# Softmax division ahead of the transposes in a hybrid encoder: weights divided on GpSimd, value products with features on partitions

## The chip, the cores and the metric

The kernel runs on one core of one Trainium2 chip. The metric is the device time of one execution in microseconds, lower is better. The core has TensorE (PE in the rows, with its weight loads as PEld), VectorE (DVE), ScalarE (ACT), GpSimd (POOL) and SyncE (SP, which only starts DMAs here).

## The reference, cut to what matters

The program is one inference step of two layers for 256 prompt tokens and 32 sample tokens. Between two large feed-forward blocks each layer mixes tokens with three groups of heads; the change concerns the first group, forgetting attention of the prompt tokens:

```
def fox_block(q, k, v, cq, ck, mask):
    s = jnp.einsum('bqhd,bkhd->bhqk', q, k).astype(F32) * (HEAD_DIM ** -0.5)
    s = s + jnp.swapaxes(cq, 1, 2)[:, :, :, None] - jnp.swapaxes(ck, 1, 2)[:, :, None, :]
    s = jnp.where(mask[None, None], s, -jnp.inf)
    p = jax.nn.softmax(s, axis=-1).astype(v.dtype)
    return jnp.einsum('bhqk,bkhd->bqhd', p, v)
...
    o_fox = (o_fox.reshape(B, T, FOX_WIDTH) * jax.nn.sigmoid(fg)).astype(x.dtype)
```

It has 8 heads of 64 features; `cq` and `ck` are running sums of log forget gates; queries come in two blocks of 128, of which the first sees 128 keys and the second 256. The second group of heads (RWKV-7) carries a state of 64x64 per head through the sequence; the kernel computes it in nine chunks of 32 tokens, each of which needs the state that the one before left.

## The kernel before, in words

All tensors are feature-major: features on partitions, 288 tokens along the free axis. Each engine has one instruction stream, written by hand in program order; semaphores join them. In the part that the change touches the nine chunks of the recurrence run one after another, and the work of the forgetting heads is written between their parts. We call chunk i "step i", from 0 to 8.

A step of the recurrence is a chain of four links. TensorE multiplies the state by the chunk's vectors (L1769); VectorE adds the result to `u0` (L1206); TensorE adds two products for the new state (L1775, which needs nothing new, and L1782, which waits for `u0`); VectorE scales the old state and adds (L1213, two instructions). The next step's first product waits for that.

The forgetting heads go in four pairs p of heads 2p and 2p+1. The stages of a pair:

- `fox_scores(p)`, TensorE, L1701 and L1706: scores into PSUM banks 4 and 5, one for each head. It waits until the exponentials of the pair before have read them.
- `fox_max(h)`, VectorE, L1176: mask and row minimum of the negated scores, in two parts.
- `fox_exp(h)`, ScalarE, L691: exponentials of both parts into `pq`, with their row sums into `fm`. It waits until the transposes of head h-2 have read `pq`.
- `fox_weights(p)`, TensorE, L1731: three 128x128 transposes for each head into banks 6 and 7.
- `fox_copy(h)`, ScalarE, L701: copy of these from PSUM to `pt`.
- `fox_products(p)`, TensorE, L1743: six products of the weights (stationary, 128x128) with the values (64 columns), into bank 3, tokens on partitions.
- `fox_normed(p)`, VectorE, L1183 and L1184: reciprocal of the sums, product with them, to `otok`.
- `fox_back(p)`, TensorE, L1753: two transposes, so that features are on partitions again.
- `fox_out(p)`, VectorE, L1192: product with the gate into `hT`.

`fox_values` (L1717, copies L708) transposes the values once. Which stage stands behind which step is set by two tables named `meanwhile`, one in TensorE's stream and one in VectorE's (there with the part of the step: "u" behind L1206, "s" behind L1213). ScalarE's stream has no steps: it takes its work in the written order. `at_most` (L934) and two passes at L578 and L579 make the gate.

After step 8 TensorE computes the recurrence's outputs (L1801, then L1813), four sums for a norm (L1821), and the scores of the sample tokens (L1835), and so on to the output projection (L1882). GpSimd starts a few DMAs in this stretch.

Of the kernel before, what the change touches and what calls it, by code (L numbers as in the profile page):

```python
# [79 lines left out]
for _name, _n in (("n1", DB), ("nm", DB), ("n2", DB), ("pn", DB), ("mu", 7), ("prev", 7), ("bf", 1), ("w0", 2),  # L80
# [29 lines left out]
    fexp=16, ft_ps=8, ftc=8, fo_ps=4, fno=4, ft2=4, fo_ok=4, ss_ps=2, smx=2, sexp=4, st_ps=4, stc=4, so_ps=1,  # L110
# [19 lines left out]
def program(nc, wcol, x_in, p_in, consts_in, params_in, foxl_in, kc_in, vc_in, clf_in, srwkv_in, sret_in,  # L130
            nf_in, y_out, k_out, v_out, logf_out, shift_out, rwkv_out, ret_out):
    with ExitStack() as ctx:
# [231 lines left out]
        with nc.Block() as block:  # L364
# [42 lines left out]
            def _(pool):  # L407
                for layer in range(DEPTH):
# [42 lines left out]
                    pool.dma_start(ret_out[layer, 1], rst[:, 6, :, :]).then_inc(S["zstore"], 16)  # L451
                    pool.wait_ge(S["s_ok"], past["s_ok"] + 18)
# [14 lines left out]
            def _(act):  # L467
                n_chain = [0]
                for layer in range(DEPTH):
# [241 lines left out]
                    for p in range(4):  # L711
                        for e in range(2):
                            fox_copy(2 * p + e)
                        if p < 3:
                            for e in range(2):
                                fox_exp(2 * p + 2 + e)
# [100 lines left out]
            def _(dve):  # L817
                n_chain = [0]
                for layer in range(DEPTH):
# [359 lines left out]
                    def fox_normed(p):  # L1179

                        dve.wait_ge(S["fo_ps"], past["fo_ps"] + p + 1)
                        total = 12 + 4 * (p % 2)
                        link(dve.reciprocal(fm[:, 20:24], fm[:, total:total + 4]))  # L1183
                        dve.tensor_tensor(otok, bank[3][:, 0:256].rearrange("p (a d) -> p a d", a=4),  # L1184
                                          fm[:, 20:24].unsqueeze(2).to_broadcast([P, 4, HD]), ALU.mult).then_inc(S["fno"], 1)

                    def fox_out(p):

                        if p == 0:
                            dve.wait_ge(S["fg_ok"], past["fg_ok"] + 1)  # L1190
                        dve.wait_ge(S["ft2"], past["ft2"] + p + 1)
                        dve.tensor_tensor(hT[:, p, 0:TP], bank[3][:, 256:512], fg[:, p, 0:TP], ALU.mult).then_inc(S["fo_ok"], 1)  # L1192

                    meanwhile = {(0, "u"): [(fox_max, 0)], (0, "s"): [(fox_max, 1)], (1, "s"): [(at_most, fg)],
                                 (2, "u"): [(fox_max, 2)], (2, "s"): [(fox_max, 3)], (3, "u"): [(fox_normed, 0)],
                                 (4, "u"): [(fox_out, 0)], (4, "s"): [(fox_max, 4)], (5, "u"): [(fox_max, 5)],
                                 (5, "s"): [(fox_normed, 1)], (6, "s"): [(fox_out, 1)], (7, "u"): [(fox_max, 6)],
# [945 lines left out]
```

## Time and profile before

| what | us |
|---|---|
| median of 3 runs | 1439.85 (1438.88 to 1444.85) |
| the profiled execution, its own time | 1437.9 |
| its span | 1436.1 |
| TensorE busy | 1367.6 (95%) |
| VectorE busy | 864.2 (60%) |
| ScalarE busy | 597.0 (42%) |
| GpSimd busy | 49.3 (3%) |

The span is what the trace covers; the profiled execution took 1.8 us more. TensorE is busy nearly throughout, most of it in the feed-forward blocks. The stretch with the nine steps stands once in each layer, at 382 to 429 us and at 1096 to 1137 us of the span.

### The profile page before, as it was taken

The page shows a single profiled execution, that of the slowest core. Times are in us where ns is not written, and L with a number is a line of the kernel's source. Part 1 is how long each engine was busy: PE and PEld are TensorE (multiplying, and loading weights), DVE is VectorE, ACT ScalarE, POOL GpSimd, SP SyncE. Part 2 cuts the span into 40 slices and gives each one's busy share as a digit, 9 for nine tenths or more (in the row PEclk, how much of TensorE's full clock was granted, in tenths as well). Part 3 has the DMA queues.
Part 4 walks back from the last instruction along what each step waited for, and adds up shares of the span by engine and source line. Part 5 has one row for each costly group of instructions (what it writes and reads, how often), then busy time and mean ns, then how long its engine had stood idle before and what let it go on. Part 6 is the DMA issues. An engine that isn't in the chain of part 4 may idle for free.

```text
span 1436.1 us, 29222 instructions
## 1 busy us (share of the span) xinstructions
PE 1367.6 (95%) x12544; PEld 1317.7 (92%) x12544; DVE 864.2 (60%) x1365; ACT 597.0 (42%) x845; POOL 49.3 (3%) x71
## 2 busy tenths in 40 slices
PE   6999999998898999999999999999989899999997
PEld 6999999898777999999989999998977699999996
DVE  5766536796346566653766664467853565766546
ACT  5443434533326544433544343335333364443333
POOL 1000000003100000000000000000031100000000
PEclk9999999999779999999999999999997899999999
DMA  8444443434103344444444444523432035444440
GB/s 315 166 175 157 165 171 122 147 122 152 65 14 118 147 162 160 175 154 169 151 151 176 154 168 173 178 90 120 163 110 64 14 118 199 153 175 156 167 146 34
DMA packets 31328, 205.29 MB, mean 143 GB/s; under 512 B 4312, under 2 KB 5864, under 8 KB 7544
## 3 DMA queue, kind: packets, MB, share of 16 engines
q1 hardware_dynamic: 28672, 195.62, 37.9%
q0 software_dynamic: 2560, 8.26, 1.7%
q8 instruction: 75, 1.23, 0.3%
q14 instruction: 21, 0.17, 0.0%
HBM read 199.77 MB, written 4.10 MB: 142 GB/s over the span
## 4 chain that ended last, share of the span: by engine, by line
PE 88%; DVE 4%; ACT 4%; issue 2%; DMA 1%; POOL 0%; SPq 0%; DVEq 0%; ACTq 0%
PE banks L1390 40%; PE banks L1413 19%; PE banks L1465 11%; PE banks L1919 3%; PE banks L1882 3%; PE banks L1887 1%; PE banks L1701 1%; PE banks L1900 1%; PE banks L1743 1%; PE banks L1643 1%; PE banks L1821 1%; PE banks L1706 1%; ACT split_h L572 1%; PE banks L1631 1%; PE banks L1731 0%
## 5 line engine op out<-in xcount | busy, mean ns | idle before, releaser
L1390 PE MATMUL banks<-split_x,split_w 128*128 128x288 f32 x4224 | 570.5, 297 | 16.2 <-ACT split_x L492 11.8
L1390 PEld LDWEIGHTS banks<-split_x,split_w 128*128 128x128 f32 x4224 | 567.4, 190 | 18.8 <-issue 11.7
L844 DVE TENSOR_TENSOR split_w<-wc,split_w 128x2048 fp32r<-128x2048 f32 x139 | 318.6, 2292 | 346.5 <-ACT split_w L508 346.5
L508 ACT ACTIVATE split_w<-wc 128x2048 fp32r<-128x2048 f32 x139 | 266.4, 1916 | 401.0 <-PE banks L1390 207.4
L1413 PE MATMUL banks<-split_x,split_w 128*128 (+1 forms) x2112 | 282.3, 295 | 0.0
L1413 PEld LDWEIGHTS banks<-split_x,split_w 128*128 128x128 f32 x2112 | 281.8, 188 | 0.0
L1465 PE MATMUL banks<-split_h,split_x 128*128 128x288 f32 x752 | 115.7, 301 | 5.7 <-ACT split_x L566 4.2
L1465 PEld LDWEIGHTS banks<-split_h,split_x 128*128 128x128 f32 x752 | 105.9, 191 | 9.0 <-DVE zT L939 5.4
L566 ACT ACTIVATE split_x<-wc 128x1024 fp32r<-128x1024 f32 x62 | 65.1, 1057 | 112.2 <-PE banks L1465 97.2
L533 ACT ACTIVATE et<-hT 128x288 f32<-128x288 f32 x88 | 35.5, 445 | 110.4 <-DVE hT L863 110.3
L1465 PE MATMUL banks<-split_x 128*128 128x288 f32 x496 | 76.9, 298 | 0.0
L1465 PEld LDWEIGHTS banks<-split_x 128*128 128x128 f32 x496 | 70.2, 191 | 0.0
L1919 PE MATMUL banks<-split_x,split_w 128*128 128x288 f32 x384 | 53.0, 297 | 0.0
L1919 PEld LDWEIGHTS banks<-split_x,split_w 128*128 128x128 f32 x384 | 51.7, 189 | 1.1 <-ACT split_x L784 1.1
L939 DVE TENSOR_TENSOR zT<-banks,rs 128x288 f32<-128x288 f32 x62 | 28.1, 454 | 33.0 <-PE banks L1465 24.1
L1465 PE MATMUL banks<-split_h,split_e 128*128 128x288 f32 x240 | 38.2, 302 | 7.5 <-DVE split_e L930 7.5
L868 DVE SCALAR_TENSOR_TENSOR et<-et,hT 128x288 f32<-128x288 f32 x88 | 36.4, 455 | 12.6 <-ACT et L533 9.1
L930 DVE TENSOR_TENSOR split_x<-wc,split_x 128x1024 fp32r<-128x1024 f32 x32 | 39.0, 1218 | 7.8 <-ACT split_x L566 7.8
L874 DVE SCALAR_TENSOR_TENSOR et<-et,banks 128x288 f32<-128x288 f32 x88 | 39.3, 450 | 4.8 <-PE banks L1390 3.5
L1465 PEld LDWEIGHTS banks<-split_h,split_e 128*128 128x128 f32 x240 | 34.4, 193 | 8.4 <-DVE split_e L930 8.4
L930 DVE TENSOR_TENSOR split_e<-wc,split_x 128x1024 fp32r<-128x1024 f32 x30 | 36.5, 1217 | 6.8 <-ACT split_x L566 6.8
L863 DVE TENSOR_TENSOR hT<-banks,rs 128x288 f32<-128x288 f32 x88 | 35.9, 449 | 5.9 <-ACT rs L487 5.9
(290 smaller groups left out, 1194.6 us busy)
## 6 DMA issues: line engine op xcount, KB each, us to landing
wc<-wcol SPq DMA_DIRECT2D x182, 1024.0 KB, 4.8
arena<-kc_in POOLq DMA_DIRECT2D x8, 256.0 KB, 3.5
arena<-vc_in POOLq DMA_DIRECT2D x2, 1024.0 KB, 7.5
con<-consts_in SPq DMA_DIRECT2D x1, 1830.0 KB
xT<-x_in SPq DMA_DIRECT2D x2, 576.0 KB, 4.5
k_out<-zT POOLq DMA_DIRECT2D x8, 144.0 KB, 2.5
v_out<-zT POOLq DMA_DIRECT2D x8, 144.0 KB, 2.5
y_out<-hT SPq DMA_DIRECT2D x8, 144.0 KB, 1.9
```

The lines of the kernel that those rows point to most:

```text
L508: act.activation(ws[(s + 1 - f) % 2][0], wc[:, p % RING, :], ACT.Copy).then_inc(S["cast"], 1)
L566: act.activation(zw[n % 2][0], z_raw(n), ACT.Copy).then_inc(S["zcast"], 1)
L844: dve.tensor_tensor(lo, wc[:, (POS_FFN[f] + s) % RING, :], hi, ALU.subtract).then_inc(S["wlo"], 1)
L863: dve.tensor_tensor(half[:, q % 2, :], bank[2 * (q % 4)][:, 0:T], rs[:], ALU.mult)\
L868: dve.scalar_tensor_tensor(e, e, 1.0, half[:, q % 2, :], ALU.add, ALU.mult)\
L874: dve.scalar_tensor_tensor(e, e, 0.5, bank[2 * (q % 4) + 1][:, 0:T], ALU.mult, ALU.mult)\
L930: dve.tensor_tensor(lo, z_raw(n), hi, ALU.subtract).then_inc(S["zlo"], 1)
L1390: mm = pe.matmul(o, w[:, k, cs], x[:, k, :], start=(n == 0 and k == 0), stop=(n == 2 and k == DB - 1))
L1413: return pe.matmul(bank[m][:, 0:T], w[:, kk, m * 128:m * 128 + 128], rhs, start=start, stop=stop)
L1465: mm = pe.matmul(o, w[:, k, :], zh_lo(k) if second else zh_hi[:, k, :], start=(i == 0 and k == 0), stop=(i == 2 and k == DB - 1))
L1882: pe.matmul(bank[2 * s + cc][:, 0:T], hi[:, k, cc * 128:cc * 128 + 128], x[:, k, :], start=(x is oh_hi and k == 4), stop=False)
L1919: mm = pe.matmul(bank[2 * s + cc][:, 0:T], w[:, k, cc * 128:cc * 128 + 128], x[:, k, :], start=(n == 0 and k == 0), stop=(n == 2 and k == ...
```

## The change

The softmax's division moves from behind the value products to ahead of the transposes. VectorE now takes the reciprocal of a head's two sums as soon as its exponentials are there (`fox_inverse`), and GpSimd multiplies the head's exponentials by them, in place (`fox_divide`). The transposes wait for GpSimd in place of ScalarE. The value products are turned round: the values are stationary (128x64), the weights move, 256 and 128 columns at a time, and the two heads of a pair write to the two halves of bank 3's partitions. Features are then on partitions at once, so `fox_normed` and `fox_back` are gone, and `fox_out` reads the products directly. The tables give some stages other steps, and ScalarE takes the exponentials of the next pair between the copies of a pair, where it took them behind both.

```
...
         pool.dma_start(ret_out[layer, 1], rst[:, 6, :, :]).then_inc(S["zstore"], 16)
+        def fox_divide(h):
+            p, e = h // 2, h % 2
+            pool.wait_ge(S["frc"], past["frc"] + h + 1)
+            for part, (a0, a1) in enumerate(((0, 128), (128, 384))):
+                one = 20 + 4 * (p % 2) + 2 * part + e
+                done = pool.tensor_scalar(pq[:, e, a0:a1], pq[:, e, a0:a1], fm[:, one:one + 1], None, ALU.mult)
+            done.then_inc(S["fpn"], 1)
+        for h in range(FOX_H):
+            fox_divide(h)
         pool.wait_ge(S["s_ok"], past["s_ok"] + 18)
...
             for e in range(2):
+                if p < 3:
+                    fox_exp(2 * p + 2 + e)
                 fox_copy(2 * p + e)
-            if p < 3:
-                for e in range(2):
-                    fox_exp(2 * p + 2 + e)
...
-        def fox_normed(p):
-            dve.wait_ge(S["fo_ps"], past["fo_ps"] + p + 1)
-            total = 12 + 4 * (p % 2)
-            link(dve.reciprocal(fm[:, 20:24], fm[:, total:total + 4]))
-            dve.tensor_tensor(otok, bank[3][:, 0:256].rearrange("p (a d) -> p a d", a=4),
-                              fm[:, 20:24].unsqueeze(2).to_broadcast([P, 4, HD]), ALU.mult).then_inc(S["fno"], 1)
+        def fox_inverse(h):
+            p, e = h // 2, h % 2
+            dve.wait_ge(S["fexp"], past["fexp"] + 2 * h + 2)
+            at = 4 * (p % 2) + e
+            dve.reciprocal(fm[:, 20 + at:23 + at:2], fm[:, 12 + at:15 + at:2]).then_inc(S["frc"], 1)
         def fox_out(p):
             if p == 0:
                 dve.wait_ge(S["fg_ok"], past["fg_ok"] + 1)
-            dve.wait_ge(S["ft2"], past["ft2"] + p + 1)
-            dve.tensor_tensor(hT[:, p, 0:TP], bank[3][:, 256:512], fg[:, p, 0:TP], ALU.mult).then_inc(S["fo_ok"], 1)
-        meanwhile = {(0, "u"): [(fox_max, 0)], (0, "s"): [(fox_max, 1)], (1, "s"): [(at_most, fg)],
-                     (2, "u"): [(fox_max, 2)], (2, "s"): [(fox_max, 3)], (3, "u"): [(fox_normed, 0)],
-                     (4, "u"): [(fox_out, 0)], (4, "s"): [(fox_max, 4)], (5, "u"): [(fox_max, 5)],
-                     (5, "s"): [(fox_normed, 1)], (6, "s"): [(fox_out, 1)], (7, "u"): [(fox_max, 6)],
-                     (7, "s"): [(fox_max, 7)], (8, "u"): [(fox_normed, 2)], (8, "s"): [(fox_out, 2)]}
+            dve.wait_ge(S["fo_ps"], past["fo_ps"] + p + 1)
+            dve.tensor_tensor(hT[:, p, 0:TP], bank[3][:, 0:TP], fg[:, p, 0:TP], ALU.mult).then_inc(S["fo_ok"], 1)
+        meanwhile = {(0, "u"): [(fox_max, 0)], (0, "s"): [(fox_max, 1)], 
+                     (1, "s"): [(at_most, fg), (fox_inverse, 0), (fox_inverse, 1)],
+                     (2, "u"): [(fox_max, 2)], (2, "s"): [(fox_max, 3)], (3, "s"): [(fox_inverse, 2)],
+                     (4, "u"): [(fox_inverse, 3), (fox_out, 0)], (5, "u"): [(fox_max, 4)], (5, "s"): [(fox_max, 5)],
+                     (6, "u"): [(fox_inverse, 4), (fox_inverse, 5), (fox_out, 1)], (7, "u"): [(fox_max, 6)],
+                     (7, "s"): [(fox_max, 7)], (8, "u"): [(fox_inverse, 6)],
+                     (8, "s"): [(fox_inverse, 7), (fox_out, 2)]}
         dve.wait_ge(S["uac"], past["uac"] + 8)
...
         dve.tensor_copy(kc[:, :, PAST:], zT[:, Z_FK:Z_FK + 4, TP:T]).then_inc(S["kcnew"], 1)
-        fox_normed(3)
         by_chunk = ow[:, :, 0:TP].rearrange("p b (j c u) -> p c j b u", j=2, c=4)
...
                 h = 2 * p + e
-                pe.wait_ge(S["fexp"], past["fexp"] + 2 * h + 2)
+                pe.wait_ge(S["fpn"], past["fpn"] + h + 1)
                 if p:
...
                 pe.wait_ge(S["fo_ok"], past["fo_ok"] + p)
-            for e in range(2):
-                hv = slice(HD * (2 * p + e), HD * (2 * p + e) + HD)
-                for i, (q, kb) in enumerate(((0, 0), (1, 0), (1, 1))):
-                    at = 128 * q + 64 * e
-                    mm = pe.matmul(bank[3][:, at:at + HD], pt[:, e, 128 * i:128 * i + 128], vtok[:, kb, hv],
-                                   start=(kb == 0), stop=(kb == q))
+            for kb, (a0, a1) in enumerate(((0, 256), (256, 384))):
+                for e in range(2):
+                    hv = slice(HD * (2 * p + e), HD * (2 * p + e) + HD)
+                    mm = pe.matmul(bank[3][64 * e:64 * e + 64, 128 * kb:256], vtok[:, kb, hv], pt[:, e, a0:a1],
+                                   start=(kb == 0), stop=(kb == 1), skip_group_check=True)
             mm.then_inc(S["fo_ps"], 1)
-        def fox_back(p):
-            pe.wait_ge(S["fno"], past["fno"] + p + 1)
-            both = otok.rearrange("p a d -> p (a d)")
-            for q in range(2):
-                at = 256 + 128 * q
-                mm = pe.transpose(bank[3][:, at:at + 128], both[:, 128 * q:128 * q + 128], c("ident"))
-            mm.then_inc(S["ft2"], 1)
         fox_scores(0)
-        meanwhile = {0: [(fox_values,)], 1: [(fox_weights, 0), (fox_scores, 1)], 2: [(fox_products, 0)],
-                     3: [(fox_back, 0), (fox_weights, 1), (fox_scores, 2)], 4: [(fox_products, 1)], 5: [],
-                     6: [(fox_back, 1), (fox_weights, 2), (fox_scores, 3)], 7: [(fox_products, 2)],
-                     8: [(fox_back, 2), (fox_weights, 3)]}
+        meanwhile = {0: [(fox_values,)], 1: [(fox_scores, 1)], 2: [(fox_weights, 0)], 3: [(fox_products, 0)],
+                     4: [(fox_scores, 2), (fox_weights, 1)], 5: [(fox_products, 1)],
+                     6: [(fox_scores, 3), (fox_weights, 2)], 7: [(fox_products, 2)], 8: []}
         for i in range(NCH):
...
         mm.then_inc(S["o_in"], 1)
-        fox_products(3)
+        fox_weights(3)
         pe.wait_ge(S["o_in"], past["o_in"] + 1)
...
             mm.then_inc(S["o_ps"], 1)
-        fox_back(3)
+        fox_products(3)
```

ScalarE's stream from the copies of pair 0 to the exponentials of pair 2, before (L701 is a copy, L691 an exponential; 128x128 and 128x256 are a head's two parts):

```order
L701 ACTIVATE arena<-banks 128x384 [waits ft_ps] x2
L691 ACTIVATE arena<-banks,arena 128x128 [waits fmx,ft_ps]
L691 ACTIVATE arena<-banks,arena 128x256
L691 ACTIVATE arena<-banks,arena 128x128 [waits fmx,ft_ps]
L691 ACTIVATE arena<-banks,arena 128x256
L701 ACTIVATE arena<-banks 128x384 [waits fo_ps,ft_ps] x2
L691 ACTIVATE arena<-banks,arena 128x128 [waits fmx,ft_ps]
L691 ACTIVATE arena<-banks,arena 128x256
```

The same place after the change (L713 is a copy, L703 an exponential):

```order
L703 ACTIVATE arena<-banks,arena 128x128 [waits fmx,ft_ps]
L703 ACTIVATE arena<-banks,arena 128x256
L713 ACTIVATE arena<-banks 128x384 [waits ft_ps]
L703 ACTIVATE arena<-banks,arena 128x128 [waits fmx,ft_ps]
L703 ACTIVATE arena<-banks,arena 128x256
L713 ACTIVATE arena<-banks 128x384 [waits ft_ps]
L703 ACTIVATE arena<-banks,arena 128x128 [waits fmx,ft_ps]
L703 ACTIVATE arena<-banks,arena 128x256
L713 ACTIVATE arena<-banks 128x384 [waits fo_ps,ft_ps]
```

Before, both copies of pair 0 come ahead of all exponentials of pair 1. Now each copy stands behind the exponentials of the head two further on: the copy of head 0 behind those of head 2, and so on to the last row, the copy of head 2, behind those of head 4.

TensorE's stream from the products of pair 1 to step 6, before (L1769, L1775 and L1782 are a step, L1743 the products):

```order
L1743 MATMUL banks<-arena 128x64 [waits fo_ok,ftc]
L1743 MATMUL banks<-arena 128x64 x5
L1769 MATMUL banks<-extra,arena 32x64 [waits s_ok]
L1769 MATMUL banks<-extra,arena 32x64 x3
L1775 MATMUL banks<-extra 64x64 x4
L1782 MATMUL banks<-arena,extra 64x64 [waits u_ok]
L1782 MATMUL banks<-arena,extra 64x64 x3
L1769 MATMUL banks<-extra,arena 32x64 [waits s_ok]
L1769 MATMUL banks<-extra,arena 32x64 x3
L1775 MATMUL banks<-extra 64x64 x4
```

After the change, from step 5 on (L1753 are now the products):

```order
L1769 MATMUL banks<-extra,arena 32x64 [waits s_ok]
L1769 MATMUL banks<-extra,arena 32x64 x3
L1775 MATMUL banks<-extra 64x64 x4
L1782 MATMUL banks<-arena,extra 64x64 [waits u_ok]
L1782 MATMUL banks<-arena,extra 64x64 x3
L1753 MATMUL banks<-arena 64x256 [waits fo_ok,ftc]
L1753 MATMUL banks<-arena 64x256
L1753 MATMUL banks<-arena 64x128 x2
L1769 MATMUL banks<-extra,arena 32x64 [waits s_ok]
L1769 MATMUL banks<-extra,arena 32x64 x3
```

Before, the products of pair 1 come ahead of step 5, and step 6 follows it directly. After, step 5 is the first five rows, and the products stand between it and step 6. The products of pair 2 stand between steps 7 and 8 in both kernels.

TensorE's stream behind step 8, before (L1801 and L1813 are the recurrence's outputs, L1753 the transposes back, L1821 the norm's sums):

```order
L1801 MATMUL banks<-arena,extra 64x32 x2
L1801 MATMUL banks<-arena 64x32 x2
L1743 MATMUL banks<-arena 128x64 [waits fo_ok,ftc]
L1743 MATMUL banks<-arena 128x64 x5
L1813 MATMUL banks<-arena,extra 64x32 [waits o_in]
L1813 MATMUL banks<-arena,extra 64x32 x35
L1753 MATMUL banks<-con,arena 128x128 [waits fno]
L1753 MATMUL banks<-con,arena 128x128
L1821 MATMUL banks<-arena,con 128x288 [waits ftc]
L1821 MATMUL banks<-arena,con 128x288
```

After the change (L1742 are the transposes of the weights, L1753 the products):

```order
L1801 MATMUL banks<-arena,extra 64x32 x2
L1801 MATMUL banks<-arena 64x32 x2
L1742 MATMUL banks<-con,arena 128x128 [waits ftc,fpn]
L1742 MATMUL banks<-con,arena 128x128 x2
L1742 MATMUL banks<-con,arena 128x128 [waits ftc,fpn]
L1742 MATMUL banks<-con,arena 128x128 x2
L1813 MATMUL banks<-arena,extra 64x32 [waits o_in]
L1813 MATMUL banks<-arena,extra 64x32 x35
L1753 MATMUL banks<-arena 64x256 [waits fo_ok,ftc]
L1753 MATMUL banks<-arena 64x256
L1753 MATMUL banks<-arena 64x128 x2
L1821 MATMUL banks<-arena,con 128x288 [waits ftc]
```

The last pair's transposes have moved from ahead of L1801 to behind it, and its products from ahead of L1813 to behind it.

## Rows read from the trace of the kernel before

**Rows 1.** Windows of layer 0, then layer 1: length, busy time of each engine, clock, DMA

```profile
core 0: us, PE busy (x) PEld busy (x) DVE busy (x) ACT busy (x) POOL busy (x), PEclk, DMA share, GB/s
418.60:428.80 10.20, 10.20 (x98) 8.88 (x95) 4.30 (x12) 1.06 (x1) 0.54 (x1) 0.55 0.10 32
382.36:428.80 46.44, 42.15 (x582) 34.45 (x581) 20.88 (x82) 15.68 (x46) 1.61 (x3) 0.83 0.04 12
...
1123.10:1136.80 13.70, 13.19 (x310) 11.32 (x307) 7.57 (x29) 3.75 (x11) 1.61 (x3) 1.00 0.06 16
1095.64:1136.80 41.16, 37.97 (x582) 31.03 (x581) 20.02 (x81) 15.68 (x46) 1.61 (x3) 0.92 0.04 13
```

**Rows 2.** Waits of TensorE, 382.3 to 428.8 us: total, times, longest

```profile
PE banks L1801 <- issue: 1.2, 1, 1.2
PE banks L1731 <- ACT arena L708: 0.8, 1, 0.8
PE banks L1769 <- DVE extra L1213: 0.7, 1, 0.7
```

**Rows 3.** Timeline of step 7: start, duration, engine, line, operation, idle before and releaser

```profile
410.06 0.41 PE L1769 MATMUL banks<-extra,arena 64*32 64x64 f32 x8
...
410.52 0.43 DVE L1206 TENSOR_TENSOR arena<-arena,banks 32x256 f32<-32x256 f32 x1 [4.73 <-PE banks L1769]
410.98 0.30 DVE L1176 CUSTOM_DVE_ANT_0 banks<-banks,con 128x128 f32<-128x128 f32 x1
...
411.38 1.55 PE L1743 MATMUL banks<-arena 128*128 128x64 f32 x12
...
411.88 0.37 ACT L691 ACTIVATE arena<-banks,arena 128x128 f32<-128x128 f32 x1 [4.75 <-DVE arena L1176]
...
412.86 0.41 PE L1769 MATMUL banks<-extra,arena 64*32 64x64 f32 x8
```

**Rows 4.** Timeline of step 1 on ScalarE and VectorE, and a reciprocal of step 6

```profile
385.01 0.37 ACT L691 ACTIVATE arena<-banks,arena 128x128 f32<-128x128 f32 x1
...
385.81 1.52 ACT L708 ACTIVATE arena<-banks 128x512 f32<-128x512 f32 x3
386.12 0.45 PE L1782 MATMUL banks<-arena,extra 32*64 32x64 f32 x8
...
387.00 0.75 DVE L934 TENSOR_SCALAR zT<-zT 128x1152 f32<-128x1152 f32 x1
...
402.73 0.17 DVE L1183 RECIPROCAL arena<-arena 128x4 f32<-128x4 f32 x1
```

**Rows 5.** All copies L701: duration ns min/median/max, first and last start

```profile
L701 ACT ACTIVATE arena<-banks x16: 471/488/490, 390.1 to 1128.9; 128x384 f32<-128x384 f32 x16
```

**Rows 6.** Timeline of TensorE behind step 3, at the full clock

```profile
394.77 0.44 PE L1753 MATMUL banks<-con,arena 128*128 128x128 f32 x2 [0.22 <-DVE arena L1184]
...
395.04 0.82 PE L1731 MATMUL banks<-con,arena 128*128 128x128 f32 x6
...
395.70 1.48 PE L1701 MATMUL banks<-foxR,foxL 128*128 128x128 f32 x8
...
397.11 0.93 PE L1706 MATMUL banks<-zT 64*128 64x128 f32 x8
397.96 0.41 PE L1769 MATMUL banks<-extra,arena 64*32 64x64 f32 x8
```

**Rows 7.** Timeline of TensorE behind step 6, at half the clock

```profile
405.12 1.49 PE L1731 MATMUL banks<-con,arena 128*128 128x128 f32 x6
...
406.40 2.77 PE L1701 MATMUL banks<-foxR,foxL 128*128 128x128 f32 x8
```

**Rows 8.** Timeline of TensorE, layer 0: products in column and row tiles; layer 1: full tiles

```profile
432.57 1.15 PE L1843 MATMUL banks<-arena,zT 64*32 64x512 f32 x32
...
1134.86 2.11 PE L1821 MATMUL banks<-arena,con 128*128 128x288 f32 x8
```

**Rows 9.** GpSimd's multiplications by a per-partition scalar: duration ns min/median/max

```profile
L443 POOL TENSOR_SCALAR arena<-arena,par x4: 993/1195/1395, 350.2 to 1062.8; 128x288 f32<-128x288 f32 x4
```

More of the change, by code:

```diff
@@ L109 @@
     rsd=10, ro_ps=2, ro_ok=3, rgate=2, fu_ok=1, fl_ok=1, lgf_ok=1, fc_ok=3, vt_ps=3, vtc=3, fs_ps=8, fmx=16,
-    fexp=16, ft_ps=8, ftc=8, fo_ps=4, fno=4, ft2=4, fo_ok=4, ss_ps=2, smx=2, sexp=4, st_ps=4, stc=4, so_ps=1,
+    fexp=16, ft_ps=8, ftc=8, frc=8, fpn=8, fo_ps=4, fo_ok=4, ss_ps=2, smx=2, sexp=4, st_ps=4, stc=4, so_ps=1,
     son=1, sot=1, so_ok=1, gpre=2, kcnew=1, mixout=1, pchain=4, rwkv_done=1, ret_done=1, ocast=4, olo=4, oh_hi=3, oh_lo=3, pj_ps=8,
```

## The prediction

> **What bounds the kernel now.** The profile page has TensorE busy for 95% of the span, so I looked first at who ends its waits, and then at the one stretch that the change touches. There the windows show 42.15 us of TensorE work in 46.44 us in layer 0, and 37.97 in 41.16 in layer 1 [rows 1]. Its waits by releaser are few: 0.8 us for ScalarE's copies of the values, 0.7 for the state of step 6, and 1.2 of issue in L1801 [rows 2]. So VectorE and ScalarE are hidden, and TensorE's own time sets the length, if it isn't made to wait. The two layers do the same work with 5.3 us of difference; 1.2 of it is the issue gap, and about 4.1 is the clock: behind step 8 layer 0 has a granted clock of 0.55, close to the lower level of 1.2 GHz, and layer 1 has 1.00, which is 2.4 GHz [rows 1]. Both layers fall to the lower level once more, at step 6. There a pair's scores take 3.66 us (406.40 to 410.06) where they take 2.26 at the full clock (395.70 to 397.96), and the transposes 1.49 against 0.82 [rows 3, 6, 7]. With step 6 itself that is some 2.5 us in each layer. What a delay here costs, the end pays: behind the stretch TensorE goes on in written order, and no DMA limits what follows.
>
> **What TensorE no longer does.** The transposes back take 0.27 us a pair (394.77 to 395.04) [rows 6], 1.1 us a layer. The products take 1.48 (411.38 to 412.86) [rows 3]. The new ones have as many moving columns in each pass as L1706, which runs in two row halves and takes 0.85 (397.11 to 397.96) [rows 6]: four matmuls, two of 256 and two of 128 columns, two passes each. If the two column halves do not run side by side, the price per column of L1821 holds, 2304 columns in 2.11 us, and 1536 columns take 1.4 [rows 8]. But L1843, in four column strips and two row halves, moves 16 passes of 512 and 16 of 32 columns in 1.15 us, a seventh of that price [rows 8], which row halves alone don't give. I take 0.86; 1.4 would add 4.3 us over both layers. So TensorE's work falls by 4 x 0.62 + 1.1 = 3.6 us a layer.
>
> **Waits that go.** The transposes of pair 0 no longer come ahead of the copies of the values (0.8), step 6 no longer follows step 5 directly (0.7) [rows 2], and `fox_back` no longer waits for `fox_normed` (0.2 at step 3 [rows 6], and as much behind step 8). A view counts idle from a matmul's modelled end, about 0.1 us late, so by starts it is 2.1 us a layer.
>
> **Waits that come.** The main one follows from ScalarE's new order. At step 5 TensorE stands at the products of pair 1 and needs the copies of heads 2 and 3; those stand behind the exponentials of heads 4 and 5, whose row minima VectorE takes in this same step. From the start of a step's first product to the first exponential of its scores is 1.82 us in the trace (410.06 to 411.88, over the add at 410.52 and the minimum at 410.98) [rows 3]. Exponentials hold ScalarE 0.80 (385.01 to 385.81) [rows 4], a copy takes 0.49 [rows 5]. So the copies are there 1.82 + 0.80 + 0.49 + 0.80 + 0.49 = 4.40 us after the step's start. TensorE has finished the step after 1.32 (410.06 to 411.38) [rows 3] and waits 3.1 us. The same stands at step 7 for the products of pair 2, which before ran at once, because the copies of pair 2 came ahead of the exponentials of pair 3. Behind the waiting products stands the next step of the recurrence, and behind that everything: 6.2 us a layer. At step 3 the exponentials come from a step earlier, and I count nothing.
>
> The second is GpSimd. One multiplication of 128x288 takes 0.993 at least [rows 9]. A head needs 128 and 256 columns in two instructions: 1.32 if all the time goes by columns, 1.99 if all goes by instruction. I take the middle, 1.65, and 3.3 for a pair. The first pair's reciprocals follow `at_most`, which ends at 387.75; with 0.2 for a reciprocal the divides end at 391.25. TensorE is at the second head's transposes at 386.12 + 0.4 + 2.26 for the scores + 1.32 for step 2 + 0.33 for the first head = 390.4 [rows 4], so it waits 0.9. For pair 2, from the start of step 6: add 0.46, next on VectorE 0.46, reciprocal 0.2, divides 3.3, together 4.4; TensorE takes 1.32 + 2.26 + 0.33 = 3.9 and waits 0.5. Pair 1's divides lie beside step 4 and the scores of pair 2, pair 3's beside L1801. With 1.99 the two waits grow by 0.7 each, 2.8 us over both layers; with 1.32 they nearly vanish, and the copy at step 3 takes half of that back. The reciprocals on VectorE replace those of `fox_normed` and lie beside TensorE's work.
>
> The Trainium skill (GPSIMD Engine Reference, 4.1 Engine selection) gives elementwise work to VectorE and calls GpSimd roughly line-rate for one input; 384 elements at its 1.2 GHz would be an estimate of 0.32 us a head, and the sum would be 2 us smaller. The trace's 0.993 for 288 speaks against that figure [rows 9].
>
> Third, L1801 used to stand behind the last pair's transposes, which covered the last state update. Now it follows step 8 and waits for it like step 6 did, 0.6 [rows 2]. GpSimd's output DMAs now stand behind the divides, and nobody waits for them in this stretch.
>
> **Sum at the clocks of before.** Per layer 6.2 + 0.9 + 0.5 + 0.6 = 8.2 us of new waits, less 2.1 of old ones, less 3.6 of work: 2.5. Both layers: +5 us.
>
> **The clock.** TensorE stands still for 3 us twice a layer, with only small tiles around it. In layer 0 of before the clock fell after the gap in L1801 and stayed low to 428.8; in layer 1, without the gap, it stayed full [rows 1, 2]. The wait at step 7 is followed by short work and then L1801, in both layers. So I expect the low clock behind step 8 in both: +4.1 in layer 1, and the last pair's transposes, which now lie there, +0.7 in each. The low clock around step 6 I expect as before, on the scores of pair 3 and the transposes of pair 2, which still stand there; TensorE is then so slow that it no longer meets the 0.5 of the divide, -1.0 over both layers. That makes +4.5. In all 1437.9 + 5 + 4.5 = 1447.4 for the profiled execution's own time. Its 1437.9 is 1.95 under the median of the runs, so **1449.5 us** is the forecast.
>
> **Rivals.** *The clock stays as it was* (chance 0.27): the waits come, but layer 1 keeps its full clock behind step 8. For it: there was no fall in layer 1, although TensorE's work was much the same. Then +5, 1445.
>
> *Full clock throughout, not slower* (0.07): scores of pair 1 now come without a wait, so wide matmuls stand closer together in the first steps, and the clock may hold in both layers. That takes back 2.5 in each layer and 4.1 in layer 0, 9.1 in all, against +5: 1436. It decides where both low stretches of layer 0 are gone; one alone doesn't. Against it: the new waits are the longest that TensorE would have in the stretch.
>
> *GpSimd is too slow* (0.09): another of the same multiplications took 1.395 [rows 9]. At that, a head costs 2.8 and a pair 5.6. Every pair's transposes then wait, by 2.3 us more a pair less what was covered, about 7 us a layer more: 1449.5 + 14 less some 2 of clock, 1461. It sets in at about 2 us a head; below that only two waits are touched. The Trainium skill (SBUF — State Buffer, Who interferes with whom) has GpSimd blocked only by VectorE instructions with two SBUF inputs or in a two-port mode. By that rule the divides would run free, since VectorE's work in the steps reads PSUM and one SBUF tensor, and this rival would fall.
>
> My own case, waits and low clock, has 0.5, with its own range 1445 to 1456; the remaining 0.07 is for what I don't see. A measurement of this kernel tells about 0.5%, 7.2 us, from no change. The own case is over that with 0.42 of its 0.5; slow divides all; the clock-as-before case mostly under it, 0.06 over, with products in series (1449) among the reasons. That gives slower 0.57, the same 0.37, faster 0.06. For the range I leave out the full-clock case and the slow end of the divides: 1441 to 1460.
>
> **What would show it.** Idle of about 3 us ahead of L1753 behind steps 5 and 7, ended by ScalarE's copy L713; products at about 0.86 us; 1.3 to 2.0 us of GpSimd a head; short waits of L1742 for L459; L1801 waiting about 0.6 for L1225; the granted clock near 0.5 behind step 8 in both layers. The forecast is wrong if the products wait under 2 us, if the clock differs, or if the divides exceed 2 us.

## The result, and the profile after

The changed kernel takes **1453.7 us** (median of 6 runs, 1449.2 to 1457.0) against 1440.3 for the kernel before (6 runs): ratio over the runs 1.0074, 95% interval 1.0048 to 1.0100 (the two medians alone stand at 1.0093). It is slower by some 0.7 to 0.9%. A second batch of 6 runs gave 1455.6 and 1.0093 (1.0062 to 1.0125). The forecast was 1449.5, with 1441 to 1460 as its range. The profiled execution after has an own time of 1449.61 us and a span of 1447.8, with a mean clock of 0.959; before it was 1437.9, 1436.1 and 0.968.

TensorE's waits of the changed kernel, 382.3 to 445 us, layer 0 (total, times, longest); layer 1 reads the same:

```profile
PE banks L1753 <- ACT arena L713: 6.4, 3, 3.0
...
PE banks L1801 <- DVE extra L1225: 0.6, 1, 0.6
...
PE banks L1742 <- POOL arena L459: 0.3, 1, 0.3
```

These stand against [rows 2]. The old waits of [rows 2] are gone, and TensorE now waits for ScalarE's copies, twice for 3 us and once, at step 3, for 0.44. The timeline around step 5, layer 0, tells why, and ends with the next step of the recurrence (start, duration, engine, line, operation, idle before and releaser):

```profile
401.20 0.87 PE L1742 MATMUL banks<-con,arena 128*128 128x128 f32 x6
...
402.00 0.41 PE L1769 MATMUL banks<-extra,arena 64*32 64x64 f32 x8
...
403.81 0.37 ACT L703 ACTIVATE arena<-banks,arena 128x128 f32<-128x128 f32 x1 [8.73 <-DVE arena L1187]
...
404.62 0.49 ACT L713 ACTIVATE arena<-banks 128x384 f32<-128x384 f32 x1
404.99 0.38 ACT L703 ACTIVATE arena<-banks,arena 128x128 f32<-128x128 f32 x1
...
405.78 0.51 ACT L713 ACTIVATE arena<-banks 128x384 f32<-128x384 f32 x1
...
406.34 0.87 PE L1753 MATMUL banks<-arena 128*64 128x256 f32 x8 [2.96 <-ACT arena L713]
...
407.14 0.64 PE L1769 MATMUL banks<-extra,arena 64*32 64x64 f32 x8
```

The transposes of pair 1 end when step 5 begins, at 402.0, and ScalarE stands idle; yet the copies of heads 2 and 3 come only at 404.62 and 405.78, behind the exponentials of heads 4 and 5, whose minima VectorE takes during step 5. The products take 406.34 to 407.14, 0.80 us. The next step already runs at the lower clock: 0.64 for what took 0.41 at 402.00.

The same wait at step 7, GpSimd's divides for the last pair, and the short wait for the last state:

```profile
418.79 1.55 PE L1753 MATMUL banks<-arena 128*64 128x256 f32 x8 [2.96 <-ACT arena L713]
...
421.53 3.00 POOL L459 TENSOR_SCALAR arena<-arena 128x128 f32<-128x128 f32 x4 [10.00 <-DVE arena L1195]
...
422.68 0.47 PE L1801 MATMUL banks<-arena,extra 32*64 32x32 f32 x16 [0.58 <-DVE extra L1225]
```

The windows of the whole stretch, from step 0 to the sample scores, in both layers, of the kernel after; its columns are those of [rows 1]:

```profile
384.20:435.44 51.24, 42.97 (x559) 32.14 (x558) 18.45 (x81) 15.16 (x46) 13.63 (x19) 0.73 0.05 17
1097.97:1148.68 50.71, 42.43 (x558) 31.72 (x557) 18.52 (x81) 15.15 (x46) 13.63 (x19) 0.73 0.06 19
```

Layer 1 in four pieces: up to the products behind the first long wait; steps 6 to 7; around the second wait; from its products on:

```profile
1097.97:1120.00 22.03, 17.45 (x220) 12.25 (x218) 10.38 (x48) 10.63 (x33) 6.01 (x8) 0.93 0.06 22
1120.00:1128.20 8.20, 8.20 (x64) 6.05 (x62) 1.73 (x7) 0.00 (x0) 2.99 (x4) 0.55 0.00 0
1128.20:1132.50 4.30, 1.18 (x18) 0.72 (x15) 2.00 (x11) 2.48 (x10) 0.00 (x0) 0.80 0.02 4
1132.50:1148.68 16.18, 15.60 (x270) 12.70 (x267) 4.40 (x16) 2.04 (x3) 4.63 (x7) 0.53 0.10 28
```

And the same stretch of the kernel before, both layers, cut at the same instructions:

```profile
1095.64:1136.81 41.17, 37.98 (x583) 31.04 (x582) 20.03 (x81) 15.68 (x46) 1.61 (x3) 0.92 0.04 13
382.36:428.84 46.48, 42.19 (x582) 34.45 (x581) 20.92 (x82) 15.68 (x46) 1.61 (x3) 0.83 0.04 12
```

How to read them: length less TensorE's busy time is its idle time. It was 4.3 and 3.2 us and is 8.3 and 8.3, so the waits cost 9.1 us over both layers. The busy time went up too, from 80.2 to 85.4, although the work went down. That is the clock: in layer 1 the waits are followed by 8.2 us at 0.55 and 16.2 us at 0.53. The stretches are 14.3 us longer; the rest of the program was 2.6 us shorter in this pair of executions.

### The profile page after: what moved, and what is told of

The parts are those of the page before. It is cut to its first block, busy times and chain, and to the rows that moved or that the text cites. A ratio compares the mean times of both kernels' runs of the same rounds, so it can differ in the third digit from the quotient of the medians.

```text
span 1447.8 us, 29158 instructions
## 1 busy us (share of the span) xinstructions
PE 1370.7 (95%) x12496; PEld 1313.8 (91%) x12496; DVE 860.9 (59%) x1365; ACT 596.5 (41%) x845; POOL 73.1 (5%) x103
## 4 chain that ended last, share of the span: by engine, by line
PE 88%; ACT 4%; DVE 4%; issue 2%; DMA 0%; SPq 0%; DVEq 0%; ACTq 0%
PE banks L1401 39%; PE banks L1424 19%; PE banks L1476 11%; PE banks L1919 3%; PE banks L1882 2%; PE banks L1712 1%; PE banks L1887 1%; PE banks L1900 1%; ACT arena L703 1%; PE banks L1753 1%; PE banks L1654 1%; PE banks L1821 1%; PE banks L1642 1%; PE banks L1717 1%; PE banks L1813 1%
## 5 line engine op out<-in xcount | busy, mean ns | idle before, releaser
L1401 PE MATMUL banks<-split_x,split_w 128*128 128x288 f32 x4224 | 571.1, 298 | 16.1 <-ACT split_x L504 11.7
L1401 PEld LDWEIGHTS banks<-split_x,split_w 128*128 128x128 f32 x4224 | 567.9, 190 | 18.8 <-issue 11.7
```

The lines of the kernel that those rows point to most:

```text
L1401: mm = pe.matmul(o, w[:, k, cs], x[:, k, :], start=(n == 0 and k == 0), stop=(n == 2 and k == DB - 1))
```

## The experiments

**Where the time goes: the order on ScalarE.** In the changed kernel ScalarE's stream alone goes back to the order of before:

```
             for e in range(2):
-                if p < 3:
-                    fox_exp(2 * p + 2 + e)
                 fox_copy(2 * p + e)
+            if p < 3:
+                for e in range(2):
+                    fox_exp(2 * p + 2 + e)
```

> The changed kernel with one edit: ScalarE takes both copies of a pair ahead of the next pair's exponentials, as before the change. Theory A (the loss comes from the products of pairs 1 and 2 waiting 3.0 us each for copies that stand behind exponentials): both waits vanish in both layers, 12 us less than the changed kernel at equal clocks, near 1441 if the clock stays low where it is low now, near 1432 if the clock recovers with the waits; so 1430 to 1441, at or under the kernel before. Theory B (GpSimd's divides set the time of the steps): the waits move to the transposes, under 4 us less, near 1450. Theory C (the low clock alone is the loss and comes from the mix of small tiles, not from the waits): idle goes but the granted clock of the stretch stays near 0.74.

Measured: 1430.7 us (6 runs, 1426.9 to 1433.9), ratio to before 0.9916 (0.9898 to 0.9935). That is Theory A, at the low end of its range. Four lines in another order take some 23 us off the changed kernel and make it faster than before. The products stand right behind step 5 and wait for nothing:

```profile
401.94 0.45 PE L1783 MATMUL banks<-arena,extra 32*64 32x64 f32 x8
...
402.32 0.87 PE L1754 MATMUL banks<-arena 128*64 128x256 f32 x8
...
402.82 0.37 ACT L703 ACTIVATE arena<-banks,arena 128x128 f32<-128x128 f32 x1 [1.16 <-DVE arena L1188]
```

The stretches are 40.85 and 40.33 us. That is 20.8 us less than after over both layers: 11.6 less idle and 9.2 less busy time, with the same work. The low clock behind step 8 is still there:

```profile
1091.58:1117.50 25.92, 24.06 (x320) 17.26 (x318) 14.49 (x67) 13.24 (x42) 9.08 (x13) 1.00 0.02 4
1117.50:1131.91 14.41, 13.83 (x247) 11.39 (x241) 4.95 (x15) 2.45 (x5) 4.46 (x7) 0.53 0.10 32
```

**The rival: GpSimd.** The changed kernel without GpSimd's multiplications; the division of the softmax is left out:

```
-        for h in range(FOX_H):
-            fox_divide(h)
...
-                pe.wait_ge(S["fpn"], past["fpn"] + h + 1)
+                pe.wait_ge(S["fexp"], past["fexp"] + 2 * h + 2)
```

> The changed kernel without GpSimd's multiplications: the transposes wait for the exponentials, so the attention weights stay undivided (this leaves the softmax's division out). Theory A: only 0.3 us of waits a layer goes, the products still wait 3.0 us twice; within 2 us of the changed kernel, and slower than the kernel before by about as much as it. Theory B: the loss against the kernel before goes, 1440 or less.

Measured: 1455.3 us (4 runs), ratio 1.0099 (1.0075 to 1.0122): Theory A, as slow as with the divides. The waits for the copies stay, at this kernel's lines:

```profile
PE banks L1751 <- ACT arena L711: 6.7, 3, 3.0
```

GpSimd isn't the cause of the loss.

**The clock apart from the waits.** The changed kernel with six spare matmuls of 256 columns ahead of the products of pairs 1 and 2, where TensorE stood still. Nobody reads their results:

```
+            if p in (1, 2):
+                for _ in range(6):
+                    pe.matmul(bank[0][:, 256:512], c("ident"), foxR[:, 0:256], start=True, stop=True)
```

> The changed kernel with six spare matmuls of 256 columns (0.43 us each at the full clock, 2.6 us in all, into an unused part of a PSUM bank) written ahead of the products of pairs 1 and 2, where TensorE would wait 3.0 us. It adds work and takes no wait away. Theory A with the waits as the cause of the low clock: the granted clock stays at 1.00 through the scores of pair 3 and behind step 8, and the stretch gets shorter by up to the price of the low clock (about 2 us at step 6 and 5 us behind step 8 in each layer), 1440 to 1448. If the low clock comes from the small tiles and not from the waits: no gain, 1450 to 1458, with the granted clock low behind step 8 as in the changed kernel.

Measured: 1444.3 us (10 runs, 1437.9 to 1452.7), ratio 1.0026 (1.0004 to 1.0047). More work in the same order, and 9.4 us faster by the medians, inside the range of Theory A. In layer 1 the clock stayed full from end to end:

```profile
1098.85:1139.88 41.03, 38.04 (x583) 28.51 (x581) 18.55 (x81) 15.02 (x46) 13.57 (x19) 1.00 0.05 20
```

41.03 against the 50.71 of after. The filling doesn't bring the copies forward: the products of pair 1 start 20.54 us behind the start of step 0 (20.55 in after), those of pair 2 start 4.35 behind that of step 7 (4.36 in after). So the low clock costs at least 9.7 us there. In layer 0 it fell all the same (50.42 us, clock 0.80), but not at the filled places: once at 397.7 us, in step 4 and ahead of the first of them, and once at 421.6, in L1801 behind step 8. So the filling kept the clock up where it stood, in four places of four; it doesn't prevent a fall elsewhere.

**One wait of the two.** The changed kernel with ScalarE's copies of pair 1 moved ahead; those of pair 2 stay:

```
+            if p == 1:
+                fox_copy(2)
+                fox_copy(3)
             for e in range(2):
                 if p < 3:
                     fox_exp(2 * p + 2 + e)
-                fox_copy(2 * p + e)
+                if p != 1:
+                    fox_copy(2 * p + e)
```

> The changed kernel with one half of its order mended: ScalarE copies heads 2 and 3 ahead of the exponentials of heads 4 and 5; the copies of heads 4 and 5 stay behind the next exponentials. Theory A (each of the two waits costs its own 3 us and a share of the clock): one wait of 3.0 us a layer is left, at the products of pair 2; of the 23 us between the changed kernel and the one with all copies first, half is back: 1440 to 1445. Rival B (one wait is enough to bring the low clock over the rest of the stretch, since the recurrence follows it): only the 6 us of the waits come back, 1446 to 1449. Rival C (the first wait alone costs the clock): 1434 to 1438.

Measured: 1444.1 us (10 runs, 1440.2 to 1449.9), ratio 1.0021 (1.0003 to 1.0040): inside the range of Theory A. In layer 1:

```profile
PE banks L1757 <- ACT arena L713: 3.2, 2, 3.0
```

In both layers the clock falls inside the wait that is left and stays low for 17 us; in layer 1 it also fell at 1107.9, for 10 us, where no long wait stands. With no, one and two long waits in each layer the kernel takes 1430.7, 1444.1 and 1453.7. By these medians a wait costs 13 or 10 us over both layers, by the ratios 15 or 8, and 23 for the two together is the firmer figure. Standing still is 6 of each.

**The moved steps.** The kernel with the copies first, with before's tables of steps:

```
-        meanwhile = {0: [(fox_values,)], 1: [(fox_scores, 1)], 2: [(fox_weights, 0)], 3: [(fox_products, 0)],
-                     4: [(fox_scores, 2), (fox_weights, 1)], 5: [(fox_products, 1)],
-                     6: [(fox_scores, 3), (fox_weights, 2)], 7: [(fox_products, 2)], 8: []}
+        meanwhile = {0: [(fox_values,)], 1: [(fox_weights, 0), (fox_scores, 1)], 2: [(fox_products, 0)],
+                     3: [(fox_weights, 1), (fox_scores, 2)], 4: [(fox_products, 1)], 5: [],
+                     6: [(fox_weights, 2), (fox_scores, 3)], 7: [(fox_products, 2)], 8: [(fox_weights, 3)]}
```

The last pair's stages go back in the same way, and so does VectorE's table, except that it has the reciprocals directly behind the minima of their pair, a place that before doesn't use.

> The changed kernel's data flow (division ahead of the transposes, values stationary, no transposes back) at the steps of the kernel before: both tables as they were, copies ahead of exponentials, reciprocals directly behind the minima that they follow. Theory A with the moved steps as what pays: VectorE now waits for exponentials inside the steps, and the transposes for GpSimd; a replay of the rows gives 6 us a layer more than e1_copies_first, so 1442 to 1450. If the smaller work of TensorE (3.5 us a layer) were what counts, it would be as fast as e1_copies_first.

Measured: 1450.4 us (4 runs), ratio 1.0064 (1.0040 to 1.0088), 20 us above the run with the new tables, and just over the 1442 to 1450 expected. Its waits in layer 0:

```profile
PE banks L1784 <- DVE arena L1219: 4.6, 6, 1.5
PE banks L1743 <- POOL arena L459: 2.3, 3, 0.9
PE banks L1771 <- DVE extra L1226: 0.8, 1, 0.8
```

With the old tables the reciprocals and divides have less cover. VectorE waits 3.1 us in this layer for the exponentials that its reciprocals need (0.4 with the new tables), its part of the recurrence is late, and the transposes wait for GpSimd. TensorE's smaller work alone brings nothing here; it needs steps that cover the new stages. Other places for the reciprocals in the old tables were not tested.

**The divides without the long waits.** The kernel with the copies first, less GpSimd's multiplications; the division is left out, by the edit of the second experiment.

> The kernel with the copies first, and without GpSimd's multiplications; it leaves out the division of the softmax, so its output differs by that. Theory A (GpSimd's divides are hidden also where the copies no longer wait; only the 0.3 us wait of L1743 for GpSimd goes): within 2 us of the kernel with the copies first, 1429 to 1432, with the transposes then waiting for the exponentials instead. Rival B (with the long waits gone, the divides have become the next limit, or they slow VectorE and ScalarE by sharing the memory): 1421 to 1427.

Measured: 1428.0 us (6 runs, 1421.5 to 1434.2), ratio 0.9915 (0.9883 to 0.9948), between the two ranges and by its ratio the same as with them (0.9916). So GpSimd's 12 us a layer are hidden, or all but a few us over both layers, which the interval doesn't exclude.

**The column halves.** The kernel with the copies first, with the two loops of the products changed over:

```
-            for kb, (a0, a1) in enumerate(((0, 256), (256, 384))):
-                for e in range(2):
+            for e in range(2):
+                for kb, (a0, a1) in enumerate(((0, 256), (256, 384))):
```

> The kernel with the copies first, with the two loops of the products changed over: both matmuls of a head (256 and 128 columns) come one behind the other, then those of the other head, where they alternated between the two column halves of TensorE. Theory A (the halves run side by side only because neighbouring instructions go to different halves): the products of a pair take up to 1.4 us in place of 0.80, 0.6 more for each of four pairs in two layers, together about 5 us: 1434 to 1437. Rival B (each pass is spread over the halves whatever the order): 0.80 as before, and 1430 to 1432. Rival C (in between: only the two middle matmuls overlap): about 1.1 us a pair, 1432 to 1434.

Measured: 1430.6 us (8 runs), ratio 0.9929 (0.9905 to 0.9954). The timeline behind step 3:

```profile
395.32 0.88 PE L1754 MATMUL banks<-arena 128*64 128x256 f32 x8
396.12 0.41 PE L1770 MATMUL banks<-extra,arena 64*32 64x64 f32 x8
```

395.32 to 396.12 is 0.80 us, as with the halves alternating: Rival B. The trace's single records show the overlap itself: the eight passes start in four twos, 13 ns apart within a two, and from the second two on the next comes 0.216 us behind 256 columns and 0.109 behind 128. That is the price per column of the full tiles of L1821 (0.242 us for 288 columns), for two passes at once. This run also gave a layer with the full clock throughout:

```profile
384.90:422.07 37.17, 33.85 (x558) 25.07 (x557) 18.54 (x81) 15.70 (x46) 13.59 (x19) 0.95 0.06 21
1088.18:1122.61 34.43, 32.00 (x559) 24.12 (x558) 18.54 (x81) 15.59 (x46) 13.59 (x19) 1.00 0.07 26
```

So TensorE's work in the stretch is 32.0 us at the full clock; after does the same work in 43.0 and 42.4.

**Filling the tail.** The kernel with the copies first, with three spare matmuls behind the products of pair 2 and two ahead of L1801's wait, of the kind shown above.

> The kernel with the ScalarE copies ahead of the next pair's exponentials (1430.7 us median) still falls to the lower clock behind step 8 in both layers, although no product waits there. This run adds three spare matmuls of 256 columns behind the products of pair 2 and two ahead of L1801, whose results nobody reads. Theory A (the low clock behind step 8 comes from the short gaps and the small tiles around L1801): the clock stays at its upper level there, which gives back about 4 us a layer, less 1.3 to 2 us a layer of added matmuls: 1424 to 1428. Rival B (it comes from what TensorE did over the longer stretch before, and a little filling at that place changes nothing): the clock falls all the same, and the added work makes it 1433 to 1436.

Measured: 1431.9 us (9 runs, 1428.3 to 1435.4), ratio 0.9941 (0.9922 to 0.9960). No gain over the run without them, so neither theory holds as put: layer 1 was at the full clock (36.31 us), layer 0 fell to the lower one (42.99 us, clock 0.88). The spare matmuls add 2.45 us of busy time a layer (34.45 against 32.00). With the 4.9 that the low clock costs in layer 0 that is 9.8 us over both layers. Without them the low clock alone costs 12.2 and 9.0 in the two profiles of the kernel with the copies first, and 1.9 in that of the run with the loops changed over.

**Do the places of the low clock belong to the kernel?** Three kernels were profiled once more, unchanged: before, after, and the one with the copies first.

> The kernel before once more, unchanged, for a second profile. The question is whether the places at which the clock falls belong to the kernel or to the single execution. Theory A (they belong to the kernel's order): low clock around step 6 in both layers and behind step 8 in layer 0 alone, stretches of 46.5 and 41.2 us within 1 us. Rival B (they are drawn anew in every execution, with a share that depends on the kernel): the stretches differ from those by several us, between 38.7 (full clock throughout) and 48.

> The changed kernel once more, for a second profile and more executions. Theory A (the order sets the places of the low clock): stretches of 51.2 and 50.7 us within 1 us, low behind step 8 in both layers. Rival B (drawn anew): the waits of 3.0 us stand in both layers as before, and the stretches move by several us between 40.6 (full clock) and 53. Median of the time in both cases 1450 to 1456.

> The kernel with the copies first once more. Theory A: stretches of 40.9 and 40.3 us with the low clock behind step 8, within 1 us. Rival B: no wait of L1754 in either layer, and a length anywhere between 34.4 us (full clock, as the variant with the product loops changed over had it) and 42. Median 1428 to 1433, 8 to 13 us under the kernel before.

The windows of both layers, before, after and with the copies first:

```profile
385.83:433.08 47.25, 42.89 (x582) 35.17 (x581) 20.19 (x81) 15.81 (x46) 1.61 (x3) 0.82 0.05 17
1096.13:1141.90 45.77, 42.69 (x582) 34.73 (x581) 20.96 (x82) 15.81 (x46) 1.61 (x3) 0.82 0.07 24
```

```profile
385.66:436.22 50.56, 42.29 (x558) 31.62 (x557) 18.46 (x81) 15.13 (x46) 13.59 (x19) 0.73 0.06 19
1099.32:1149.68 50.36, 42.09 (x558) 31.40 (x557) 18.44 (x81) 15.13 (x46) 13.59 (x19) 0.73 0.06 21
```

```profile
383.92:423.80 39.88, 36.28 (x559) 27.05 (x557) 18.84 (x81) 15.71 (x46) 13.59 (x19) 0.87 0.08 26
1087.11:1126.23 39.12, 36.68 (x559) 27.44 (x557) 19.44 (x82) 15.70 (x46) 13.59 (x19) 0.87 0.07 23
```

After repeats (Theory A): four stretches between 50.4 and 51.2 us, each with 27.3 us at the lower clock. Every long wait has a fall of the clock, seven of the eight inside the wait and one 0.8 us behind its end. Before doesn't: its layer 1 took 41.17 us in one execution and 45.77 in the other, where the clock also fell behind step 8 and once more early on; it was low for 6.8 us in the one and for 16 to 17 in the other three stretches. With the copies first the length goes from 34.4 (in the run with the loops changed over) to 40.9. The times: 1444.1 (1 run) for before, 1455.6 for after, 1428.0 (4 runs, 1424.9 to 1431.1) with the copies first, ratio 0.9899 (0.9853 to 0.9945).

## Why the prediction was right, and which of its terms was not

**Right in the main: the waits behind ScalarE's copies.** Forecast 3.1 us each at steps 5 and 7, measured 2.96, 2.96 in layer 0 and 2.97, 2.96 in layer 1. The chain is the one worked out: minimum, exponential, copy, exponential, copy. That these waits cause the slowdown is shown by taking them away: 23 us go with them (0.9 of it is the short wait at step 3, which the same edit takes away).

**Right: TensorE's work.** Products 0.80 for 0.86; with four transposes back at 0.27 that is 3.8 us a layer less, forecast 3.6. The column halves run side by side whatever the order of the instructions. L1801 waits 0.6 as said.

**The divides: too dear.** Forecast 1.65 us a head, measured 1.50 (3.00 for a pair, all through). Pair 0's transposes wait 0.3, forecast 0.9, and pair 2's don't, as expected at the low clock. The 0.5 that the forecast puts there at the full clock isn't seen either: with the waits filled, layer 1, these transposes take 1.00 us (1123.87 to 1124.87) for 0.80. The Trainium skill's line-rate figure (GPSIMD Engine Reference, 4.1 Engine selection), an estimated 0.32 a head, is far from the 1.50 here; the trace's older multiplications of 288 columns were the better guide. The Trainium skill's other rule (SBUF — State Buffer, Who interferes with whom), that VectorE instructions with at most one SBUF input, outside the two-port modes, don't contend with GpSimd, agrees with the changed kernel's steps: VectorE is busy 18.54 us in the stretch with the divides (1088.18 to 1122.61 above), and just as long in the run with the copies first and no divides:

```profile
1084.79:1124.93 40.14, 37.82 (x557) 28.66 (x552) 18.54 (x81) 15.59 (x46) 1.61 (x3) 0.83 0.07 21
```

It isn't so beside every VectorE instruction. In the run with the old tables `at_most`, which goes from SBUF to SBUF, runs beside a divide in both layers. There a multiplication of 256 columns takes 1.33 us where all others take 0.91 to 0.93, and `at_most` 0.85 where it takes 0.75 otherwise:

```profile
388.38 3.40 POOL L459 TENSOR_SCALAR arena<-arena 128x128 f32<-128x128 f32 x4 [6.21 <-DVE arena L1196]
...
390.69 0.85 DVE L946 TENSOR_SCALAR zT<-zT 128x1152 f32<-128x1152 f32 x1
```

The new tables have `at_most` ahead of the first divide, so the changed kernel never meets this.

**Step 3, "I count nothing":** it waits 0.44 us in each layer for the copy of head 1.

**The waits in sum.** Forecast for both layers: 2 x (8.2 - 2.1), less 1.0 for pair 2, so 11.2 us more idle time. Measured 9.1: 1.2 less for the divides, 0.6 less for the four long waits, 0.9 more at step 3, and 1.2 less because the issue gap in L1801 of [rows 2] isn't there in after. That adds up. At the clocks of before, work and waits thus make +1.5 us (-7.6 and +9.1), not the +5 of the forecast.

**The mis-sized term: the clock.** Forecast +4.5, of which 1.0 was the wait of pair 2 that goes, so +5.5 of slower work. Of the 32.0 us at full clock, after makes 43.0 and 42.4: the low clock costs 11.0 and 10.4, and in the second profile 10.3 and 10.1. Before has 3.8 more work, 35.8 by this reckoning, and lost 6.4 and 2.2, in the second profile 7.1 and 6.9. The difference for both layers is 12.8 us in the first pair of profiles and 6.4 in the second. Two steps of the forecast failed. "The low clock around step 6 I expect as before": it now comes with the wait behind step 5. In three of the four stretches it begins inside the wait and lasts 10.2 us, and the products and step 6 are slow as well. In the fourth, layer 0 of the first profile, it begins at 407.14, behind the products, and lasts 6.8 us; that layer had another 3.4 us low at step 4, ahead of any long wait, where the scores took 2.86 us (397.48 to 400.34) for 1.51 at the full clock. And the second fall, put behind step 8, begins in the wait behind step 7 and lasts 17.1 us in all four stretches, where layer 0 of before had 10.2 at 0.55 [rows 1]. On the other side, "+4.1 in layer 1" was reckoned from a layer that happened to stay at the full clock: in before's second profile it fell there too. One profile is one draw of that.

**The total.** Work -7.6, waits +9.1, clock +12.8: +14.3 in the stretches of the first pair, +11.7 in its own time, and 13.4 between the medians. The forecast for the profiled execution had -7.2, +11.2 and +5.5. That it came within 2.2 us of the measured 1449.61 is in part luck: the clock was 7.3 us too cheap, work and waits 2.5 too dear, and the rest of the program happened to be 2.6 shorter. The second pair has -7.6, +9.1 and +6.4, 7.9 in all, and 6.4 in its own time, which was 1444.06 (over before's median) and 1450.45 (under after's). How the medians' 13.4 divides between clock in these stretches and elsewhere isn't settled by two profiles of each.

**The rivals.** *Clock as before* fell: the low clock is longer in all four stretches of after than in any of before. *Full clock throughout* fell: no stretch of after stayed at the full clock. Its sum wasn't tested as a whole; an estimate from the figures above, 32.0 of work and 8.3 of waits in each layer, is 80.6 us for both stretches, 7 less than before where the forecast had 4. *GpSimd too slow* fell with 1.50 a head and with the run without divides. What I didn't forecast is that the change holds a gain of some 10 us, which the order of four lines on another engine hides: 1430.7 with the copies first.

## What to carry to other kernels

When a stage gains a producer (here the divides) and another engine's stream is rewritten along with it, look for an in-order engine whose ready work (the copies) is queued behind work that comes only later (the next pair's exponentials), and put the ready work first. A stall of TensorE can cost more than its length: here four waits of 3 us came to some 22 us in all, 5 to 6 each, because the work behind them ran at the lower clock. Before counting on a clock that one profile shows, look at it in a second execution and in the other layer.

## What the runs showed of the hardware

- The granted clock in the same instructions differs between executions of one kernel: 41.17 and 45.77 us for layer 1 of before, 34.43 to 40.85 us for the stretch with the copies first (the shortest in the run with the loops changed over). With the two long waits it was low for 27.3 us every time (50.4 to 51.2 us). At the waits of about 3 us it fell in eight cases of eight, inside the wait or 0.8 us behind its end.
- The clock falls behind step 8 also without a long wait: in layer 1 of the kernel with the copies first it is 0.53 from 1117.50 on, where TensorE was busy 13.83 of 14.41 us. Much of its work there is the small tiles of L1801 and L1813. What makes the one execution fall and the other not stays open.
- Two 128x64 column halves of fp32 matmuls run side by side: 768 columns of moving data in 0.80 us a pair, also when the instructions of one half come together; the passes of the two halves start 13 ns apart then, and 7 where the instructions alternate.
- GpSimd's multiplication by a per-partition scalar takes 3.0 us for two heads of 128 and 256 columns each, 2.98 to 3.10 over all pairs of after and of the kernel with the copies first (0.60 and 0.92 us an instruction). Beside VectorE's `at_most` a pair took 3.40.
